# Two hybrid blocks on one core: three projections in 512-column matmuls, and a final normalisation bank by bank

## The reference, cut to what matters

```python
# block one (rnn mixer ya, attention mixer yb, eight heads of 128)
gates = sigmoid(g_br)                                   # two per feature
merged = gates[:, :, 0] * (ya @ w_proj_rnn) + gates[:, :, 1] * (yb @ w_proj_attn)
x = x + merged @ w_out
h = rmsnorm(x, norm2_g)
x = x + (gelu(dwconv(h @ w_up)) * (h @ w_gate)) @ w_down
# block two (sliding window attention, latent attention)
y = sigmoid(g_a) * (o_a @ w_o_swa) + sigmoid(g_b) * (o_b @ w_o_mla)
x = x + y @ w_out
h = rmsnorm_2(x, ffn_norm_g)
x = x + (silu(h @ w_gate) * (h @ w_up)) @ w_down
return rmsnorm_2(x, final_norm_g)
```

## Time and profile before

| what | value |
|---|---|
| median of three runs | 815.15 us (814.81 to 815.32) |
| the profiled execution | 815.03 us |
| its span (first to last instruction or transfer) | 813.2 us |
| TensorE matmuls | 801.6 us busy, 5274 |
| VectorE | 600.7 us busy, 777 |
| ScalarE | 457.4 us busy, 615 |
| GpSimd | 85.8 us busy, 94 |
| granted TensorE clock | 0.999 of full speed |
| DMA | 141 MB, 173 GB/s over the span |

### The profile page before, as it was taken

How to read it: one execution, slowest core, us unless ns; L and a number is a source line. 1 busy time by engine, 2 the same in 40 slices (tenths; PEclk the granted TensorE clock), 3 DMA queues, 4 the chain that set the end, 5 groups by cost and what they waited for, 6 DMA issues and landing times.

```text
span 813.2 us, 13489 instructions
## 1 busy us (share of the span) xinstructions
PE 801.6 (99%) x5274; PEld 733.5 (90%) x5274; DVE 600.7 (74%) x777; ACT 457.4 (56%) x615; POOL 85.8 (11%) x94
## 2 busy tenths in 40 slices
PE   8999999999999999999999999999999999999996
PEld 8998889999999899999999899789999888888885
DVE  5994898676567897778878777777787856666663
ACT  6669856665335644454444766677546554454443
POOL 2330231000022000000000450500013000000000
PEclk9999999999999999999999999999999999999999
DMA  8754555444545454554544542433445555555521
GB/s 298 252 183 156 185 200 208 156 140 140 187 156 207 158 207 161 200 206 161 200 160 176 214 162 104 150 110 108 153 149 191 208 181 185 198 189 178 201 103 52
DMA packets 22588, 140.97 MB, mean 173 GB/s; under 512 B 3474, under 2 KB 3730, under 8 KB 6546
## 3 DMA queue, kind: packets, MB, share of 16 engines
q1 hardware_dynamic: 22258, 140.03, 47.8%
q10 hardware_dynamic: 288, 0.36, 0.2%
HBM read 139.33 MB, written 1.05 MB: 173 GB/s over the span
## 4 chain that ended last, share of the span: by engine, by line
PE 93%; DVE 2%; ACT 2%; DMA 1%; issue 1%; SPq 0%; DVEq 0%; ACTq 0%
PE pp L1414 20%; PE pp L1377 19%; PE pp L1378 19%; PE pp L1379 19%; PE pp L1416 10%; PE pp L1521 1%; PE pp L1497 1%; DMA raw<-in_slabs 1%; PE pp L1484 1%; PE pp L1507 1%; DVE wlo L848 1%; PE pp L1496 1%; PE pp L1523 1%; ACT whi L466 0%; ACT vv L827 0%
## 5 line engine op out<-in xcount | busy, mean ns | idle before, releaser
L848 DVE TENSOR_TENSOR wlo<-raw,whi 128x2048 fp32r<-128x2048 f32 x129 | 298.8, 2317 | 118.9 <-ACT whi L466 118.7
L466 ACT ACTIVATE whi<-raw 128x2048 fp32r<-128x2048 f32 x129 | 246.1, 1909 | 87.0 <-PE pp L1379 86.4
L1377 PE MATMUL pp<-ahi,whi 128*128 128x256 f32 x768 | 220.5, 287 | 2.2 <-DVE alo L863 0.8
L1414 PE MATMUL pp<-ahilo,whi 128*128 128x512 f32 x704 | 221.4, 396 | 0.0
L1379 PE MATMUL pp<-ahi,wlo 128*128 128x256 f32 x768 | 217.2, 283 | 0.0
L1378 PE MATMUL pp<-alo,whi 128*128 128x256 f32 x768 | 217.2, 283 | 0.0
L1416 PEld LDWEIGHTS pp<-ahilo,wlo 128*128 128x128 f32 x704 | 132.2, 188 | 31.1
L1377 PEld LDWEIGHTS pp<-ahi,whi 128*128 128x128 f32 x768 | 147.1, 192 | 3.9 <-issue 2.3
L1378 PEld LDWEIGHTS pp<-alo,whi 128*128 128x128 f32 x768 | 147.3, 192 | 0.1
L1379 PEld LDWEIGHTS pp<-ahi,wlo 128*128 128x128 f32 x768 | 147.2, 192 | 0.0
L1416 PE MATMUL pp<-ahilo,wlo 128*128 128x256 f32 x704 | 138.3, 278 | 0.0
(11 more groups left out here) (206 smaller groups left out, 869.9 us busy)
## 6 DMA issues: line engine op xcount, KB each, us to landing
raw<-in_slabs SPq DMA_DIRECT2D x125, 1024.0 KB, 4.8
raw<-in_slabs SPq DMA_DIRECT2D x4, 512.0 KB, 9.2
raw<-in_slabs SPq DMA_DIRECT2D x2, 832.0 KB, 5.0
raw<-in_slabs SPq DMA_DIRECT2D x2, 576.0 KB, 4.5
raw<-in_slabs SPq DMA_DIRECT2D x4, 256.0 KB, 6.0
out<-gg SPq DMA_DIRECT2D x4, 256.0 KB, 2.0
x_res<-in_xT SPq DMA_DIRECT2D x3, 256.0 KB, 6.3
gate<-in_final_norm_g SPq DMA_DIRECT2D x1, 512.0 KB, 5.9
```

Of the source, the lines that this page charges most:

```text
L466: e.activation(whi[slot][:, :], raw[slot][:, :], ACT.Copy).then_inc(hi_ready, 1)
L848: e.tensor_tensor(wlo[slot][:, :], raw[slot][:, :], whi[slot][:, :].bitcast(f32), ALU.subtract).then_inc(lo_ready, 1)
L1377: e.matmul(out, lhs[0], rhs[0], start=first, stop=False, skip_group_check=True)
L1414: e.matmul(out[:, m, :], w[m][0], ACT2[:, k, :], start=k == 0, stop=False, skip_group_check=True)
```

## The change

1. **Slabs.** `wide_pair(s)` names the twelve slabs of S_PA, S_OUT and S2_OUT. They go through `feature_pairs`: per k two 512-column and two 256-column matmuls into a pair of banks, 0 and 1 or 2 and 3 in turn. `bank_plan` keeps, for each group, the last users of all of its banks. The activations of S_OUT and S2_OUT get hi and lo side by side (`ACT0`).
2. **Behind a slab.** ScalarE's `cross(s)` copies the two second halves to `crossed` (in `XA`). VectorE's `both_sums` waits for it and adds the two first halves, and `branch_wide` and `residual` use the result from SBUF.
3. **The end.** The last down slab finishes one bank after the other and signals each. ScalarE loads the table of the root ahead, squares each bank as it is done, and puts the first bank's sum into the bias of the root. Of the last half's banks, VectorE takes bank 5 as before; bank 4 it only multiplies by the gain, early, and ScalarE scales it and stores it from its own queue.

```diff
+def wide_pair(s):
+
+    for base in (S_PA, S_OUT, S2_OUT):
+        if base <= s < base + 4:
+            return (s - base) % 2
+    return None
...
         if strip_of(s) is not None:
-            b = None
+            mine = (None,)
+        elif wide_pair(s) is not None:
+            mine = (2 * wide_pair(s), 2 * wide_pair(s) + 1)
...
+            mine = (g % 2,)
+        before.append([last[b] for b in mine if b in last])
+        banks.append(mine[0])
+        for b in mine:
+            last[b] = g
...
+        ahi1, alo1 = sb("ahi1", [P, KD, SEQ], f32r), sb("alo1", [P, KD, SEQ], f32r)
+        ACT0, ACT2 = (sb(n, [P, KD, 2 * SEQ], f32r) for n in ("ahilo0", "ahilo2"))
+        pairs = [(ACT0[:, :, 0:SEQ], ACT0[:, :, SEQ:2 * SEQ]), (ahi1, alo1),
+                 (ACT2[:, :, 0:SEQ], ACT2[:, :, SEQ:2 * SEQ])]
...
+        crossed = [XA[:, 512 * i:512 * i + 512].rearrange("p (m n) -> p m n", m=2) for i in range(2)]
...
+            def cross(s):
+
+                e.wait_ge(group_done, GROUP_OF[(s, 0)] + 1)
+                e.activation(crossed[wide_pair(s)], pp[wide_pair(s)][:, :, SEQ:2 * SEQ], ACT.Copy).then_inc(crosses, 1)
...
                 last = s in (S_OUT - 1, FFN1 - 1)
                 if not last and not early_att(s + 1):
                     pre(s + 3)
+                if wide_pair(s) is not None:
+                    cross(s)
                 if S_PA <= s < S_OUT:
                     mp(s - S_PA)
...
                 if s >= S2_OUT:
+                    cross(s)
                     i = s - S2_OUT
                     norm_hi(3, pcol[:, FFNG:FFNG + KD], pairs[2][0], (2 * i, 2 * i + 1))
                     squares(3, i)
...
+            def square_sum(h, c):
+
+                e.wait_ge(down_bank, 4 + 2 * h + c + 1)
+                e.activation(VV[:, 0:512], ps[2 + 2 * h + c][:, :], ACT.Square,
+                             accum_out=fin[:, 2 * h + c:2 * h + c + 1]).then_inc(fin_sq, 1)
+                e.wait_ge(fin_sq, 2 * h + c + 1)
+
+            e.activation(root2[:, 0:1], epst[:, :], ACT.Sqrt)
             for h in range(HALVES):
-                e.wait_ge(down_bank, 4 + h + 1)
-                for c in range(2):
-                    ins = e.activation(VV[:, 0:512], ps[2 + 2 * h + c][:, :], ACT.Square,
-                                       accum_out=fin[:, 2 * h + c:2 * h + c + 1])
-                    link(ins)
-                link(e.activation(fin2[:, h:h + 1], fin[:, 2 * h:2 * h + 1], ACT.Identity,
-                                  bias=fin[:, 2 * h + 1:2 * h + 2]))
-                e.activation(fin2[:, 2 + h:3 + h], fin2[:, h:h + 1], ACT.Sqrt, bias=epst[:, :],
+                square_sum(h, 0)
+                e.activation(fin2[:, h:h + 1], fin[:, 2 * h:2 * h + 1], ACT.Identity, bias=epst[:, :],
+                             scale=1.0 / D).then_inc(fin_part, 1)
+                square_sum(h, 1)
+                e.wait_ge(fin_part, h + 1)
+                e.activation(fin2[:, 2 + h:3 + h], fin[:, 2 * h + 1:2 * h + 2], ACT.Sqrt, bias=fin2[:, h:h + 1],
                              scale=1.0 / D).then_inc(fin_root, 1)
+            e.wait_ge(fin_r, 2)
+            e.wait_ge(y_gained, 1)
+            e.activation(outp[:, 1, 0:512], outp[:, 1, 0:512], ACT.Copy, scale=finr[:, 1:2]).then_inc(y_scaled, 1)
+            e.wait_ge(y_scaled, 1)
+            e.dma_start(t["out"][0][P:2 * P, 0:512], outp[:, 1, 0:512]).then_inc(out_done, 16)
...
+            def both_sums(s):
+
+                n = [x for x in range(SLABS) if wide_pair(x) is not None].index(s)
+                x = crossed[wide_pair(s)]
+                e.wait_ge(crosses, n + 1)
+                link(e.tensor_tensor(x, pp[wide_pair(s)][:, :, 0:SEQ], x, ALU.add))
+                return x
+
+            def branch_wide(s, tiles, dst):
+
+                x = both_sums(s)
+                e.scalar_tensor_tensor(dst[:, tiles, :], dst[:, tiles, :], 1.0, x, ALU.add, ALU.mult).then_inc(
+                    bank_free["dve"], 1)
+                e.wait_ge(bank_free["dve"], emptied(GROUP_OF[(s, 0)])[1])
...
             def residual(s, i):
-                g = GROUP_OF[(s, 0)]
-                e.wait_ge(group_done, g + 1)
-
-                e.scalar_tensor_tensor(X[:, 2 * i:2 * i + 2, :], ps[BANK[g]][:, :].rearrange("p (m n) -> p m n", m=2),
-                                       0.5, X[:, 2 * i:2 * i + 2, :], ALU.mult, ALU.add).then_inc(bank_free["dve"], 1)
+
+                x = both_sums(s)
+                e.scalar_tensor_tensor(X[:, 2 * i:2 * i + 2, :], x, 0.5, X[:, 2 * i:2 * i + 2, :], ALU.mult,
+                                       ALU.add).then_inc(bank_free["dve"], 1)
...
+            def inverse(h):
+
                 e.wait_ge(fin_root, h + 1)
-                link(e.reciprocal(finr[:, h:h + 1], fin2[:, 2 + h:3 + h]))
-                for c in range(2):
-                    cols = slice(512 * c, 512 * c + 512)
-                    e.scalar_tensor_tensor(outp[:, h, cols], ps[2 + 2 * h + c][:, :], finr[:, h:h + 1],
-                                           fing[:, cols], ALU.mult, ALU.mult).then_inc(y_ready, 1)
+                e.reciprocal(finr[:, h:h + 1], fin2[:, 2 + h:3 + h]).then_inc(fin_r, 1)
+                e.wait_ge(fin_r, h + 1)
+
+            def out_bank(h, c):
+
+                cols = slice(512 * c, 512 * c + 512)
+                e.scalar_tensor_tensor(outp[:, h, cols], ps[2 + 2 * h + c][:, :], finr[:, h:h + 1],
+                                       fing[:, cols], ALU.mult, ALU.mult).then_inc(y_ready, 1)
+
+            inverse(0)
+            out_bank(0, 0)
+            out_bank(0, 1)
+            e.wait_ge(fin_sq, 3)
+            e.tensor_tensor(outp[:, 1, 0:512], ps[4][:, :], fing[:, 0:512], ALU.mult).then_inc(y_gained, 1)
+            inverse(1)
+            out_bank(1, 1)
...
+                else:
+                    for before in BEFORE[g]:
+                        who, n = emptied(before)
+                        e.wait_ge(bank_free[who], n)
...
-            def feature_pairs(out, slot, ready):
+            def feature_pairs(out, slot, act, ready):
 
                 for k in range(KD):
                     ready(k)
                     w = [weights(slot, k, slice(P * m, P * m + P), WIDE) for m in range(2)]
                     for m in range(2):
-                        e.matmul(out[:, m, :], w[m][0], ACT2[:, k, :], start=k == 0, stop=False, skip_group_check=True)
+                        e.matmul(out[:, m, :], w[m][0], act[:, k, :], start=k == 0, stop=False, skip_group_check=True)
                     for m in range(2):
-                        ins = e.matmul(out[:, m, 0:SEQ], w[m][1], ACT2[:, k, 0:SEQ], start=False, stop=k == KD - 1,
+                        ins = e.matmul(out[:, m, 0:SEQ], w[m][1], act[:, k, 0:SEQ], start=False, stop=k == KD - 1,
                                        skip_group_check=True)
                 return ins
...
+                    elif wide_pair(s) is not None:
+                        ins = feature_pairs(pp[wide_pair(s)], slot, ACT2 if S_PA <= s < S_OUT else ACT0, at)
...
+                            for i in range(4):
+                                c, k = (i // 2, i % 2) if last else (i % 2, i // 2)
+                                ins = three(ps[2 + 2 * h + c][:, :],
+                                            (acthi[:, k, P * h:P * h + P], actlo[:, k, P * h:P * h + P]),
+                                            weights(slot, k, slice(512 * c, 512 * c + 512), D), False, False)
+                                if last and (h, i) in ((0, 1), (0, 3), (1, 1)):
+                                    ins.then_inc(down_bank, 1)
                     ins.then_inc(down_bank if last else down_used, 1)
```

More of the change, by code:

```diff
@@ L132, in bank_plan @@
         if strip_of(s) is not None:
-            b = None
+            mine = (None,)
+        elif wide_pair(s) is not None:
+            mine = (2 * wide_pair(s), 2 * wide_pair(s) + 1)
         elif s < S_RI:
-            b = s % 4
+            mine = (s % 4,)
         elif s == S_RI:
-            b = i % 4
+            mine = (i % 4,)
         elif s in (S2_OSWA + 1, S2_OMLA + 1):
-            b = 2 + i
+            mine = (2 + i,)
         else:
[L141 to L144, removed]
+            mine = (g % 2,)
[3 more added lines that the diff above has]
+            last[b] = g
     return banks, before
@@ L347, in program @@
         sink_T, sink_ready = sem("sink_T"), sem("sink_ready")
+        crosses = sem("crosses")
         f_cross, f_conv, gate_scaled, f_glu, f_act, f_hi, f_lo = (sem(n) for n in (
             "f_cross", "f_conv", "gate_scaled", "f_glu", "f_act", "f_hi", "f_lo"))
-        down_bank, fin_root, y_ready = (sem(n) for n in ("down_bank", "fin_root", "y_ready"))
+        down_bank, fin_sq, fin_part, fin_root, fin_r, y_gained, y_scaled, y_ready = (sem(n) for n in (
+            "down_bank", "fin_sq", "fin_part", "fin_root", "fin_r", "y_gained", "y_scaled", "y_ready"))
         block = ctx.enter_context(nc.Block())
@@ L443, in _ @@
```

(17 more changed lines are left out.)

11 lines of the change are left out of this document (2 added, 9 removed).

## The result

The changed kernel took 818.86 us (median of 6 runs, 817.31 to 819.08), the kernel before 815.24 beside it (6 runs, 813.81 to 815.76). The ratio is 1.0041, 95% interval 1.0031 to 1.0051: slower by 2.5 to 4.2 us. The forecast was slower, 816.9, range 815.2 to 818.0; the sign is right and the size outside.

What follows compares the result with a forecast made beforehand. TensorE, busy 801.6 us of a span of 813.2, was taken as the bound. Block one +1.9, block two +1.4 and the end -1.6 gave +1.7, from the median 815.15 to 816.9 us, range 815.2 to 818.0.

Steps and rivals of the forecast that it cites:

- slab in the wide form: Each rebuilt projection slab on TensorE takes 5.57 us instead of 5.76, a saving of 0.19.
- wait at the first output projection, k=6: TensorE waits 1.4 us there for the low part from VectorE's chain behind the attention projection's last slab.
- waits at a feed-forward start: In each block TensorE waits 0.90 us at k=6 and 1.14 more for the sum of squares, 2.04 together.
- block one without the bank wait: Block one's eight slabs save 1.52 us and its waits add 1.4 and 2.04: +1.9; no bank wait was forecast.
- block two: Four slabs of the second output projection save 0.62 us, waits at the feed-forward start add 2.04: +1.4.
- bank rotation: In the projections each bank pair is free 3.9 us behind its slab and wanted 5.3 behind: cost nothing.
- the end: After TensorE's last product: 2.21 us saved by early table load, bank-by-bank finish and split products, 0.6 lost between stores: -1.6.
- a rival: TensorE restarts slowly from the five waits, 0.2 us or more each: 818 us and above, chance 0.05.
- the backlog of VectorE at the last slabs: At the attention projection's fourth slab the copy is out at 6.2 us, but VectorE is free only at 7.32.
- the first rival: GpSimd's fold and VectorE's low parts do not meet; last residual 1.03 us earlier per block: 814.8 us, chance 0.12.
- The second rival: VectorE's chain behind the last slabs ends in time at all three places, TensorE never waits: 811.4 us, chance 0.08.
- The third: The wide form saves nothing in these slabs, for instance from changing bank pairs: +2.1, 819.0 us, chance 0.05.

Runs made afterwards that it cites:

- other pair first: Changed kernel with block one's bank pairs in the other turn (banks 2 and 3 first): 818.28 us, ratio 1.0040 to the kernel before; again 817.76, 1.0025.
- new end only: Kernel before with only the change's new end, without the wide slabs: 813.74 us, ratio 0.9979 to the kernel before.
- experiment 2: Changed kernel with ScalarE's copy of the crossed halves put ahead of the weight copy in both blocks: 815.08 us, ratio 0.9998 to the kernel before.
- experiment 4: Changed kernel with the first two of three GpSimd folds of each sum of squares cut to 8 columns: 816.66 us, ratio 1.0017 to the kernel before.
- experiments 3 and 7: Kernel before plus new end, 813.74 us; change without it, 820.28. Change with other bank turn, crossed copy first, later sum matmul, ScalarE's last store moved to SyncE: 812.20.

## Why the prediction was right in sign and wrong in size

The forecast was +1.74 us on the profiled execution, and the medians show +3.6. Step by step:

| step | forecast | measured | by |
|---|---|---|---|
| slab in the wide form | 5.57 | 5.57 (weight copies, line 481, at 227.64 and 233.21) | trace after |
| wait at the first output projection, k=6 | 1.4 | 1.46 from start to start (1.29 idle) | trace after |
| waits at a feed-forward start | 0.90 + 1.14 | 0.91 + 1.02 from start to start (0.74 + 0.85 idle) | trace after |
| slower start behind each of these five waits | 0 | 5 x 0.10 (contained in the next two rows and in "the rest") | trace after |
| block one without the bank wait | +1.9 | +2.1 (D1 54.12 to 54.16) | other pair first |
| block two | +1.4 | +1.42 (D2) | trace after |
| bank rotation | 0 | +1.24 (D1) | other pair first, twice |
| the rest, from the branch to the last product | 0 | +0.2 (596.70 beside 591.70, less D1's 3.34 and D2's 1.42) | trace after |
| the end | -1.6 | -1.5 (E; -1.7 by the medians of the end alone) | new end only |

**The step that failed** stands behind the sums of the two blocks: "Each of the two bank pairs is free some 3.9 behind its slab and wanted 5.3 behind: nothing, until that cover of 1.4 is gone." That holds from pair to pair. It leaves out the passage from single banks to pairs. The rnn projection takes banks 0 and 1 in turn, so the first pair includes the bank of the slab just ended, which has no slab's time behind it. TensorE stood 1.0 us for VectorE's branch (1.24 by D1), and since the bank is asked for ahead of the attention step, that step could not cover it. It was legible before the run: `bank_plan` now records both banks' last users, and `slab` waits for the later of them ahead of the attention step. I looked at how the pairs follow each other and not at what came before the first. With this term the sum is +1.74 + 1.24 = +3.0, 818.1 from the median of before, just above the forecast's upper end of 818.0 and 0.7 short of what was measured.

**A second, smaller term was put at nothing:** the start of TensorE behind a wait. The first pair of 512-column matmuls takes 0.73 or 0.74 where the pair takes 0.63 in the earlier trace rows, and the next start comes 0.57 instead of 0.47 behind; behind the sum matmul it comes 0.35 (269.97, 270.32) instead of 0.25 (266.45, 266.70). That is 0.10 at each of the five waits, 0.5 in all, half of what a rival named. By the traces 0.5 is what is left between the sum with the bank term and the measured +3.5 (5.00 from the branch to the last matmul, less 1.48 at the end); the medians leave 0.6 to 0.7. The other differences are small and cancel: the end brought 0.1 less, the two waits for the fold were 0.1 shorter each, and the old wait in block two grew by 0.13. That block two came out at 1.42 for a forecast of 1.4 is such a cancelling, and in that part luck.

**What was right.** The place of the crossed copy behind the weight copy (experiment 2), the backlog of VectorE at the last slabs to 0.1 us, the hold-up of line 897 by GpSimd's fold, against the first rival (experiment 4), and the end with its two stores (experiments 3 and 7). The second rival, waits hidden, had against it that "the weight copy stands before the new copy in ScalarE's order"; with the other order one of the three kinds of wait does go, and of the other two 0.31 and some 0.64 us are left. The third, that the wide form saves nothing here, is out by the slab length.

## What to carry to other kernels

Look at an added copy's place in a queue before its length: here a 0.6 us step behind a 1.9 us one that waits for the same event cost 3.8 us more than ahead of it, paid where a stage hands over. Where buffers change their grain, one bank to two, look at the first use of the new grain: it needs what the old grain has only just used. And before taking 0.19 us off each of many slabs of a bound engine, reckon what each hand-over has to spare; before the change it was 1.3 us at the first output projection's k=6 (ready at 240.91, wanted at 242.2), 0.7 at the fold and nothing at block two's first output slab.

## What the runs showed that I had not expected

The form with 512-column matmuls is hardly faster for TensorE: a 256-column matmul every 0.120 us against 0.116 per 256 columns in the wide form (5.57 us for 48 such units), although a slab in it has 32 matmuls in place of 48, each with its weights to load. TensorE's first matmul pair after each wait lasts 0.1 us longer. The profile's idle time leaves out the overlap of the matmuls: a wait that costs 0.3 us from start to start may not be listed, and one listed with 1.29 costs 1.46. And the start of the kernel scatters by up to 1.4 us between executions (the same branch at 213.93 and at 215.36), more than the effect of the bank turn, so a distance between two instructions of one trace tells what medians of five and eight runs can't.
